# Band attention beside a recurrence: 60 steps in 54 rounds of each head pair instead of 56

## The reference

```
y_a = rwkv7_mix(p_r, p_k, p_v, p_wd, p_ad, ...)          # recurrence, 8 heads of 64
y_a = y_a * silu(gate_a)
y_b = chunk_attention(q_b, k_b, v_b, att_bias) * silu(gate_b)   # 8 heads of 64, 8 chunks of 64 to the left
return h + concatenate([y_a, y_b]) @ w_out

# rwkv7_mix, one step for each token:
sa    = einsum('bhvk,bhk->bhv', state, a_t)
state = state * w_t + sa * b_t + v_t * k_t
y_t   = einsum('bhvk,bhk->bhv', state, r_t)

# chunk_attention, for each chunk of 64 queries:
s = einsum('bhqd,bhkd->bhqk', q_blk, kb) * scale + bias;  p = softmax(s, masked);  out = p @ vb
```

## The kernel before

| step of the tile | PE | ACT | DVE | POOL |
|---|---|---|---|---|
| 1 | scores, L894 | copies far scores, L1720 | adds the bias to near scores, L2679 | masks, from tile 4 on |
| 2 | | | row maximum, L2690 | |
| 3 | | exp, L1727 | | |
| 4 | | | reciprocal L2696, scaling L2700 | |
| 5 | transposes, L621 of `H` | copies them, L1440 | copies the last block, L2705 | |
| 6 | product with v, L914 | copies it (odd tiles) | copies it (even tiles) | |

## Time and profile before

### The profile page before, as it was taken

One profiled execution on the slowest core, in us unless ns is written; L12 is line 12 of the kernel. 1 busy time (PEld: TensorE's weight loads), 2 busy tenths in 40 slices (PEclk: granted clock), 3 DMA queues, 4 the chain that ended last, 5 costly groups with the idle time before them and its releaser, 6 DMA issues.

```text
span 4248.0 us, 59403 instructions
## 1 busy us (share of the span) xinstructions
PE 4032.4 (95%) x26080; PEld 3206.7 (75%) x26080; DVE 1739.8 (41%) x2888; ACT 1321.2 (31%) x2315; POOL 1177.4 (28%) x613
## 2 busy tenths in 40 slices
PE   7999999989999999999999989999998999999998
PEld 4767676746998988676667767697877988888887
DVE  4363636323240248763005572231187332323353
ACT  3232324222232144562113352122275212122133
POOL 1101111002114356661222102243102523333353
PEclk9999999989999999999999999999998999999999
DMA  3001010003011121100111001120100211111111
GB/s 104 17 2 32 2 31 3 16 15 111 32 40 50 40 80 40 35 21 30 41 43 46 30 1 43 47 92 21 49 1 21 70 50 50 50 50 42 50 49 40
DMA packets 164978, 168.68 MB, mean 40 GB/s; under 512 B 8176, under 2 KB 152432, under 8 KB 164720
## 3 DMA queue, kind: packets, MB, share of 16 engines
q1 hardware_dynamic: 164720, 164.89, 12.3%
HBM read 156.48 MB, written 8.39 MB: 39 GB/s over the span
## 4 chain that ended last, share of the span: by engine, by line
PE 77%; DVE 13%; ACT 4%; issue 3%; POOL 3%; DMA 0%; POOLq 0%; SPq 0%; DVEq 0%; ACTq 0%
PE bank L633 15%; PE bank L635 15%; PE bank L634 15%; PE bank L598 5%; PE bank L621 3%; PE bank L870 3%; PE bank L1122 3%; PE bank L609 2%; PE bank L588 1%; PE bank L1137 1%; PE bank L775 1%; PE bank L1288 1%; PE bank L783 1%; POOL H L3447 1%; PE bank L1312 1%
## 5 line engine op out<-in xcount | busy, mean ns | idle before, releaser
L633 PE MATMUL bank<-XT_r,W_r 128*128 128x512 f32 x1744 | 700.8, 402 | 8.4 <-ACT BIG L1990 1.9
L634 PE MATMUL bank<-BIG_r,W_r 128*128 128x512 f32 x1624 | 632.6, 390 | 0.0
L3389 POOL TENSOR_TENSOR W_r<-W,W_r 128x2048 fp32r<-128x2048 f32 (+1 forms) x74 | 308.9, 4175 | 760.9 <-ACT W_r L1450 760.9
L635 PE MATMUL bank<-XT_r,W_r 128*128 128x512 f32 x1232 | 481.0, 390 | 0.0
L633 PE MATMUL bank<-W_r,BIG_r 128*128 128x256 f32 (+1 forms) x1280 | 418.0, 327 | 1.3 <-DVE MIX_r L2725 0.4
L633 PEld LDWEIGHTS bank<-XT_r,W_r 128*128 128x128 f32 x1744 | 328.2, 188 | 88.8 <-issue 14.2
L635 PE MATMUL bank<-W_r,BIG_r 128*128 128x256 f32 (+1 forms) x1152 | 380.4, 330 | 0.0
L634 PEld LDWEIGHTS bank<-BIG_r,W_r 128*128 128x128 f32 x1624 | 305.3, 188 | 71.9 <-issue 10.3
L598 PE MATMUL bank<-XT,W 128*128 128x512 f32 x672 | 302.3, 608 | 4.0 <-POOL MIX L3257 2.2
L635 PE MATMUL bank<-W_r,MIX_r 128*128 128x256 f32 x960 | 272.2, 284 | 0.0
L635 PEld LDWEIGHTS bank<-XT_r,W_r 128*128 128x128 f32 x1232 | 231.7, 188 | 48.6
(11 more groups left out here) (430 smaller groups left out, 7927.3 us busy)
## 6 DMA issues: line engine op xcount, KB each, us to landing
W<-w_in SPq DMA_DIRECT2D x29, 1024.0 KB, 5.5
W<-w_in_e SPq DMA_DIRECT2D x33, 512.0 KB, 6.9
MIX<-w_up SPq DMA_DIRECT2D x15, 1024.0 KB, 5.3
MIX<-w_down SPq DMA_DIRECT2D x15, 1024.0 KB, 4.9
W<-w_in_o SPq DMA_DIRECT2D x12, 1024.0 KB, 5.1
W<-w_in SPq DMA_DIRECT2D x17, 512.0 KB, 4.1
H<-x SPq DMA_DIRECT2D x16, 512.0 KB, 9.2
W<-w_out SPq DMA_DIRECT2D x7, 1024.0 KB, 5.1
```

Of the source, the lines that this page charges most:

```text
L633: E.matmul(b[:, 0:n], lh, rh, start=k == ks[0], stop=False)
L634: E.matmul(b[:, 0:n], lh, rl, start=False, stop=False)
L635: mm = E.matmul(b[:, 0:n], ll, rh, start=False, stop=k == ks[-1])
L3389: G.tensor_tensor(WLO[k % 2][:, 0:n], WSTAGE[k % 2][:, 0:n], WHI[k % 2][:, 0:n], ALU.subtract).then_inc(*s_split.mark("split", k))
```

## The change

Two edits. `pace` gives out as many band steps in a round as the ratio asks for, where it gave out one at the most; and the ratio is 60 steps to 54 rounds where it was 60 to 56.

```diff
     for r in range(-lead, rounds):
         a = next(main, "end")
-        b = next(other, "end") if r >= 0 and (r + 1) * steps // rounds > r * steps // rounds else None
+        b = None
+        for _ in range((r + 1) * steps // rounds - r * steps // rounds if r >= 0 else 0):
+            b = next(other, "end")
         if a == b == "end":
             return
         yield
...
-        RW_ROUNDS, BAND_STEPS, BAND_LEAD = 56, 60, 8
+        RW_ROUNDS, BAND_STEPS, BAND_LEAD = 54, 60, 8
```

## The result

The changed kernel is slower: a median of 4266.66 us (9 runs, 4257.77 to 4270.10) against 4243.45 for the kernel before. The ratio of the two is 1.0046, with a 95% interval of 1.0030 to 1.0063: some 20 us. The forecast was 4232, with a range of 4214 to 4252. The profiled execution took 4264.35 us, 14.6 more than that of before.

What follows compares the result with a forecast made beforehand. The prediction took TensorE as the bound, with 77% of the chain of waits; its terms summed to -11.0 us, from a median of 4243.2 us to a forecast of 4232 us, range 4214 to 4252.

Steps and rivals of the forecast that it cites:

- projections: Each pair's projections, with tiles before and after: TensorE's dense products were to cover a few changed steps, at no cost.
- the doubled rounds: Rounds taking two band steps: waits for copies, exp, scaling or bias cost 12.6 us if all on the path; half, 6.3, taken.
- last rounds: Each pair's last 20 rounds: more tile steps there, every pair losing 11.8 us as pair 0 did; 19.3 us more.
- 58/59: Band steps 58 and 59 sharing a round in three pairs: the product waits for ACT's copies, 0.73 to 0.78 us each.
- piece behind the recurrence: Band work between the recurrence's end and tile 6's transposes: 41.7 us shrink to 2, so 39.7 us go.
- its work beside the recurrence: The 23 moved band steps add their TensorE work at the high clock beside the recurrence: 14.1 us more.
- first factoring: The recurrence's first factoring, now beside q, k and v steps in every pair: loss 3.3 us for 13.1, 9.8 less.
- second factoring: The recurrence's second factoring, now beside tiles 0 to 2 in every pair: loss 4.1 us for 5.3, 1.2 less.
- The slower one: Rival, chance 0.15: in each pair's last 20 rounds TensorE waits more for VectorE and its clock falls to 0.64; 4266 us.

## Why the prediction was wrong, point by point

The terms of the sum against the two profiled executions. "Measured" is each stage's loss after, less that before, over all four pairs (the projections of pair 0 included, 11.0 before and 10.5 after). The 6.3 us for the doubled rounds are split by their place: 5.2 in the last rounds, 1.1 for 58/59 in the projections.

| term | predicted us | measured us |
|---|---|---|
| piece behind the recurrence | -39.7 | -40.7 |
| its work beside the recurrence | +14.1 | +10.3 (the rest of 58.7) |
| first factoring | -9.8 | -7.3 |
| second factoring | -1.2 | -2.4 |
| last rounds, with their doubled rounds | +24.5 | +23.5 |
| projections | 0, and 1.1 for 58/59 | +34.6 |
| sum up to the transposes of tile 6 | -11.0 | +18.0 |

The 58.7 us are by how much later the recurrence ends (917.2 for 858.5).

**The piece behind the recurrence** was right: 1.1 us are left for the 2 foreseen, and the order behind it shifted whole. Inside that term two errors cancel: from the end of tile 6's scores to its transposes it took 5.6 us and not 4.2, and the recurrence's chunk behind the scores 4.4 and not 2.5.

**The factorings** were right in mechanism and near in size. **The last rounds** were near in sum, in part by luck. The prediction took pair 0's rows for every pair, 4.9 us idle and a clock of 0.82, thus 19.6 idle and 27.6 by the clock. Measured were 31.4 idle and 20.0 by the clock, and pair 0 itself went to 8.1 idle and a clock of 0.98. VectorE's instructions ahead of the state update make waits there, as foreseen; that the doubled rounds add by pairs of steps that wait for each other was not the reason: with pairs that do not wait the loss was 55.8 us, for 57.1 with the last doubled round apart alone, and the kernel no faster.

**The projections are the step that failed.** The prediction said: "They have tiles beside them before and after, a few steps other ones. TensorE's dense products cover them. Nothing." Two things were overlooked. The doubled round 58/59 falls into the last round of the projections, where VectorE has three instructions of the recurrence still to run, and the wait that rows 7 priced at 0.75 us had been read where VectorE was idle. Its price is 3.4 us of wait, and the clock behind it. Taken apart, the loss of the four projections fell by 24.9 us (54.3 to 29.4, pair 0's 10 to 11 among both); with ScalarE's copy instead it fell by 18.4. The other is the one step by which tile 7 comes earlier: its maximum stands ahead of the recurrence's L2536, and the bonus product waits 1.5 us longer in each pair. With steps 52 to 59 there in place of 51 to 59 the loss was 16.8 and 17.3 us, no more than before. What a tile puts on VectorE was known, and the prediction used it for the last rounds alone.

With the projections so mended and all 23 steps still moved, the kernel is faster: 0.9978, some 9 us, near the 11 forecast. By other terms, though: the first factorings lose 18.0 us there, where the forecast had 3.3.

**The rivals.** The slower one gave 4266 us, and 4266.66 was measured, but by another mechanism in the main: it expected the clock of the last rounds of each pair to fall to 0.64, and it fell to 0.83 at the lowest. What it said of VectorE's instructions ahead of the recurrence's is what happened, for the most part in another stage. The number is right by chance. In the last rounds no wait is over 1.6 us, and the clock is 0.83 to 0.98; on two other schedules, dummies of 0.45 us in those pauses brought it to 1.00 in seven of eight stretches. The Trainium skill ("TensorE: Matmul & The Clock Gate", section "A second HAM failure mode: psum-queue depth-cycling") says that frequent very short idle times between groups of matmuls make the clock swing between its levels. The trace agrees that waits this short go with a lower mean clock; that waits alone decide it is not shown, since with nearly the same waits the clock was 0.98 in pair 0 and 0.83 in pair 1.

**What stays open.** Which clock a last stretch gets varies with the same schedule (pair 0: 0.98, pair 1: 0.83 in the changed kernel, with the same instructions). The ratio 60 to 56 lost 39 us there by the clock, the most of all, and no run tells why.

## What to carry to other kernels

When a second stream is woven in step by step, write down for each engine what stands in its queue beside every woven step, not only for the engine that bounds. A wait's price is that of its place: the same product behind its transposes cost 0.75 us where VectorE was free and 3.4 where it was not. Put extra steps where the other engines are free; in the last rounds, pairs of steps that do not wait for each other brought nothing. The same 60 steps in 54 rounds gave 1.0046 or 0.9937, by the choice of six steps.

## What the runs showed of the hardware

TensorE's clock in a stretch of small matmuls with waits of up to 1.6 us lay between 0.69 and 1.00, and 0.45 us of dummy matmuls per chunk (in a chunk of some 3.5 us) held it at 1.00 in seven of eight such stretches. Two of them on the schedule of before gave 0.27%, with an interval of 0.12% to 0.43%; four (0.9 us), on the schedule with doubled q, k and v steps, held it at 1.00 in two of four stretches and gave nothing that could be told from noise. The two counts were not tried on one schedule.
